# Reciprocal roots of norms computed with tokens in the partitions in a two-block transformer kernel

## What is computed

```python
def rms_norm(x, g):
    return x * lax.rsqrt(jnp.mean(x * x, axis=-1, keepdims=True) + 1e-6) * g

# block 1
mixed = sigmoid(m_gla) * (o_gla @ w_proj_gla) + sigmoid(m_nsa) * (o_nsa @ w_proj_nsa)
x = x + rms_norm(mixed @ w_out, norm_mix_post)            # "second row", norm 2
h = rms_norm(x, norm_ffn_pre)                             # norm 3
x = x + rms_norm((silu(h @ w_gate) * (h @ w_up)) @ w_down, norm_ffn_post)   # norm 4
# block 2
z = rms_norm(x, norm1_g) @ w_in_2                         # norm 5
a, gate, q, k, v = split(z)
y = depthwise_conv31(a * sigmoid(gate)) + bias
y = silu(layer_norm(y, ln_g, ln_b))                       # norm 6, 512 channels
q, k = rms_norm(q per head of 64, q_norm_g), rms_norm(k per head of 64, k_norm_g)
x = x + concat(y, neighbourhood_attention(q, k, v, rpb)) @ w_out_2
x = x + (silu(h2 @ w_gate_2) * (h2 @ w_up_2)) @ w_down_2,  h2 = rms_norm(x, norm2_g)   # norm 7
```

## Time and profile before

| | us |
|---|---|
| three runs | 1563.01, 1563.03, 1564.03 |
| median | 1563.03 |
| profiled execution, whole | 1563.54 |
| its span, first to last instruction | 1561.7 |
| TensorE busy | 1509.5 |
| VectorE busy | 672.1 |
| GpSimd busy | 653.4 |
| ScalarE busy | 588.0 |

### The profile page before, as it was taken

One profiled execution on the slowest core, in us unless ns is written; L12 is line 12 of the kernel. 1 busy time (PEld: TensorE's weight loads), 2 busy tenths in 40 slices (PEclk: granted clock), 3 DMA queues, 4 the chain that ended last, 5 costly groups with the idle time before them and its releaser, 6 DMA issues.

```text
span 1561.7 us, 20183 instructions
## 1 busy us (share of the span) xinstructions
PE 1509.5 (97%) x7270; PEld 1178.8 (75%) x7270; DVE 672.1 (43%) x1095; ACT 588.0 (38%) x906; POOL 653.4 (42%) x302
## 2 busy tenths in 40 slices
PE   7999999999999979999999997999999999999998
PEld 6888788666668847888888885666567888888887
DVE  5212445765553465334331006888736433333001
ACT  4132332744562334223332224566554332222221
POOL 3433312653134424444444552666223444444443
PEclk9999999999999979999999998999999999999999
DMA  5522211111123322333333332322113333333333
GB/s 167 170 82 76 81 46 42 53 41 42 54 56 101 92 63 82 94 96 99 101 94 97 106 108 94 122 68 64 45 41 90 96 97 94 94 94 98 106 106 108
DMA packets 40900, 135.03 MB, mean 86 GB/s; under 512 B 4468, under 2 KB 8824, under 8 KB 40584
## 3 DMA queue, kind: packets, MB, share of 16 engines
q1 hardware_dynamic: 39504, 130.56, 28.1%
q10 hardware_dynamic: 1336, 3.64, 0.8%
HBM read 132.09 MB, written 2.10 MB: 86 GB/s over the span
## 4 chain that ended last, share of the span: by engine, by line
PE 72%; issue 18%; POOL 4%; DVE 3%; ACT 2%; DMA 0%; POOLq 0%; DVEq 0%; SPq 0%; ACTq 0%
PE bank L998 18%; PE bank L1000 18%; PE bank L999 18%; POOL wL L411 3%; PE bank L1027 2%; PE bank L1028 2%; PE bank L1029 2%; PE bank L1259 2%; PE bank L1261 1%; PE bank L1260 1%; DVE bank L1874 1%; PE bank L1152 1%; PE bank L1186 1%; PE bank L1147 1%; PE bank L1254 1%
## 5 line engine op out<-in xcount | busy, mean ns | idle before, releaser
L411 POOL TENSOR_TENSOR wL<-raw,wH 128x1024 fp32r<-128x1024 f32 x235 | 573.3, 2440 | 852.9 <-ACT wH L500 673.9
L500 ACT ACTIVATE wH<-raw 128x1024 fp32r<-128x1024 f32 x209 | 221.4, 1059 | 648.6 <-PE bank L1000 594.1
L998 PE MATMUL bank<-aH,wH 128*128 128x512 f32 x1056 | 420.4, 398 | 25.4 <-DVE aL L1497 18.1
L999 PE MATMUL bank<-aL,wH 128*128 128x512 f32 x1056 | 414.0, 392 | 0.0
L1000 PE MATMUL bank<-aH,wL 128*128 128x512 f32 x1056 | 413.8, 392 | 0.0
L998 PEld LDWEIGHTS bank<-aH,wH 128*128 128x128 f32 x1056 | 199.8, 189 | 81.0 <-issue 27.0
L999 PEld LDWEIGHTS bank<-aL,wH 128*128 128x128 f32 x1056 | 200.0, 189 | 42.4 <-issue 2.0
L1000 PEld LDWEIGHTS bank<-aH,wL 128*128 128x128 f32 x1056 | 200.0, 189 | 42.1
L998 PE MATMUL bank<-fH,wH 128*128 128x512 f32 x352 | 137.3, 390 | 0.0
L999 PE MATMUL bank<-fL,wH 128*128 128x512 f32 x352 | 137.0, 389 | 0.0
L1000 PE MATMUL bank<-fH,wL 128*128 128x512 f32 x352 | 137.0, 389 | 0.0
(11 more groups left out here) (269 smaller groups left out, 1795.1 us busy)
## 6 DMA issues: line engine op xcount, KB each, us to landing
raw<-in_w SPq DMA_DIRECT2D x235, 512.0 KB, 3.5
bmk<-in_bias SPq DMA_DIRECT2D x6, 512.0 KB, 4.8
pj<-in_x SPq DMA_DIRECT2D x4, 512.0 KB, 6.4
out_x<-z2T SPq DMA_DIRECT2D x8, 256.0 KB, 3.6
ct<-in_ct ACTq DMA_DIRECT2D x3, 384.0 KB, 3.2
w1k<-in_w1k ACTq DMA_DIRECT2D x1, 1024.0 KB, 6.4
w1v<-in_w1v ACTq DMA_DIRECT2D x1, 1024.0 KB, 5.1
pv<-in_pv ACTq DMA_DIRECT2D x1, 128.5 KB, 5.6
```

What stands on the lines that cost most here:

```text
L411: pool.tensor_tensor(wL[:, c_slot, :], raw[:, c_slot, :], wH[:, c_slot, :].bitcast(F32), ALU.subtract).then_inc(sem("w_lo"), 1)
L500: act.activation(wH[:, s, :], raw[:, s, :], ACT.Copy).then_inc(sem("w_hi"), 1)
L998: pe.matmul(bank[:], hi, H[:, ka, :], start=(k == 0), stop=False)
L999: pe.matmul(bank[:], hi, L[:, ka, :], start=False, stop=False)
```

## The change

The roots of norms 2, 4 and 6 and the roots of heads are now made with tokens in the partitions. The norms 1, 3, 5 and 7 stay as they are, except that norm 5 is summed in bank 6, since bank 5 is taken.

- `token_sums` makes the squares' tile the weights and one column of ones the moving operand: for each group of 128 tokens one column of 128 sums, 128x4 for all. Ln, Exp and the Newton step (`token_root`) then work on 128x4.
- `spread_root` brings the roots back to the wide form: four transposes of a root column read as 128x128, into a bank that DVE reads in place of nr or lnr.
- The roots of heads are 128x16 (four token groups, q and k, two heads). After DVE's Newton step ACT widens them to hwide, 128x512 for q and for k (`head_roots_wide`), and `head_spread` transposes these. Its first half moves from block 1 to block 2 of its tile. The matrix `spread` and its transfer go.
- Around the LayerNorm, ACT's squares of tiles 2 and 3 stand ahead of a weight split, its root ahead of attention step 10, a weight split behind two of the four Silu; DVE takes a reciprocal between scaling passes and the copy of step 10 behind them.

The diff in its core, in this order: sums and spreads on TensorE; `head_sums`; `head_spread`; the widening and its place in the tiles of in2 on ACT, behind the weight split of the tile; ACT in the LayerNorm; the residual, the narrow root and the LayerNorm on DVE.

```diff
+            def token_sums(out, src, start, stop):
+                for t in range(TT):
+                    mm = pe.matmul(out[:, t:t + 1], src[:, t * P:(t + 1) * P], ones[:, 0:1], start=start and t == 0, stop=stop,
+                                   skip_group_check=True)
+                return mm
             def total_with_last(used, bank):
                 pe.wait_ge(sem("sq_used"), used - 1)
-                pe.matmul(bank[:], ones, ssum[:], start=True, stop=False).then_inc(sem("sq_used"), 1)
+                token_sums(bank, ssum, True, False).then_inc(sem("sq_used"), 1)
                 pe.wait_ge(sem("sq_ready"), used)
-                pe.matmul(bank[:], ones, sq[:, (used - 1) % 2, :], start=False, stop=True).then_inc(sem("sum_ready"), 1)
+                token_sums(bank, sq[:, (used - 1) % 2, :], False, True).then_inc(sem("sum_ready"), 1)
+            def spread_root(n, bank):
+                pe.wait_ge(sem("root_ready"), n)
+                for t in range(TT):
+                    mm = pe.transpose(bank[:, t * P:(t + 1) * P], root[:, t:t + 1].to_broadcast([P, P]), ident)
+                mm.then_inc(sem("root_spread"), 1)
...
             total_with_last(2 * KD, B[4])
+            spread_root(1, B[5])
...
-                pe.matmul(B[6][0:4, :], cst("sel")[:, 0:4], sq[:, 0, :], start=True, stop=False, skip_group_check=True)
-                pe.matmul(B[6][0:4, :], cst("sel")[:, NACH:NACH + 4], sq[:, 1, :], start=False, stop=True,
-                          skip_group_check=True).then_inc(sem("qk_sum"), 1)
+                for of in range(2):
+                    for t in range(TT):
+                        c = 2 * (of * TT + t)
+                        mm = pe.matmul(B[6][:, c:c + 2], sq[:, of, t * P:(t + 1) * P], cst("sel")[:, 0:2], start=True, stop=True,
+                                       skip_group_check=True)
+                mm.then_inc(sem("qk_sum"), 1)
...
                 bank = B[6 if pp < 3 else 4]
+                pe.wait_ge(sem("qk_wide"), 2 * pp + of + 1)
...
-                pe.matmul(bank[:], spread[:, of * P:(of + 1) * P], qkr[:], start=True, stop=True).then_inc(sem("qk_spread"), 1)
+                for t in range(TT):
+                    mm = pe.transpose(bank[:, t * P:(t + 1) * P], hwide[:, of, t, :], ident)
+                mm.then_inc(sem("qk_spread"), 1)
...
+            def head_roots_wide(pp):
+                act.wait_ge(sem("qk_root"), pp + 1)
+                for of in range(2):
+                    act.activation(hwide[:, of].rearrange("p t (h d) -> p t h d", h=2),
+                                   hroot[:, 2 * TT * of:2 * TT * (of + 1)].rearrange("p (t h) -> p t h", h=2).unsqueeze(3)
+                                   .to_broadcast([P, TT, 2, DH]),
+                                   ACT.Copy, scale=(DH ** -0.5, 1.0)[of]).then_inc(sem("qk_wide"), 1)
...
                 if t == 1:
-                    rsqrt(5, B[5], D, (sem("sum_ready"), 5))
+                    rsqrt(5, B[6][:], D, (sem("sum_ready"), 5))
+                if t in SPREAD_AT:
+                    head_roots_wide(SPREAD_AT[t])
...
             act.wait_ge(sem("qk_sum"), 4)
-            for j in range(2):
+            for j in range(4):
                 square(n5 + j, lambda: yT[:, j, :], wait=(sem("ln_cen"), j + 1))
+                if j == 1:
+                    head_roots_wide(3)
             ahead(p, NT2 - 1)
-            for j in range(2, 4):
-                square(n5 + j, lambda: yT[:, j, :], wait=(sem("ln_cen"), j + 1))
             q = PH["out2"]
+            rsqrt(6, narrow(B[7]), S, (sem("sum_ready"), 7), root)
             probabilities(10)
             over_sums(10)
-            rsqrt(6, B[7], S, (sem("sum_ready"), 7), r=lnr)
             probabilities(11)
             act.preload_act_table_set("silu_and_others")
             over_sums(11)
-            ahead(q, 0)
             for j in range(4):
+                if j == 2:
+                    ahead(q, 0)
...
-                    dve.scalar_tensor_tensor(tmp[:, kt % 2, :], src[:, kt, :], vec(gain, kt), nr[:], ALU.mult, ALU.mult)\
+                    dve.scalar_tensor_tensor(tmp[:, kt % 2, :], src[:, kt, :], vec(gain, kt), B[5][:], ALU.mult, ALU.mult)\
...
+            def token_root(n, bank, width):
+                dve.wait_ge(sem("ln_ready"), n)
+                link(dve.tensor_scalar(root_x, narrow(bank), 1.0 / width, EPS, ALU.mult, ALU.add))
+                dve.wait_ge(sem("nr_ready"), n)
+                link(dve.scalar_tensor_tensor(root_t, root, -0.5, root, ALU.mult, ALU.mult))
+                link(dve.tensor_tensor(root_t, root_t, root_x, ALU.mult))
+                dve.scalar_tensor_tensor(root, root_t, 1.5, root, ALU.add, ALU.mult).then_inc(sem("root_ready"), 1)
...
             masked_max(10)
             copied(9)
+            token_root(6, B[7], S)
             over_sums(10)
             normed(3, 0)
-            dve.wait_ge(sem("ln_ready"), 6)
-            link(dve.tensor_scalar(nx[:], B[7][:], 1.0 / S, EPS, ALU.mult, ALU.add))
-            newton(6, r=lnr)
             masked_max(11)
-            copied(10)
+            dve.wait_ge(sem("root_spread"), 3)
             for j in range(4):
                 dve.wait_ge(sem("ln_cen"), 4)
-                dve.tensor_tensor(yT[:, j, :], yT[:, j, :], lnr[:], ALU.mult).then_inc(sem("conv_val"), 1)
-            over_sums(11)
+                dve.tensor_tensor(yT[:, j, :], yT[:, j, :], B[7][:], ALU.mult).then_inc(sem("conv_val"), 1)
+                if j == 1:
+                    over_sums(11)
+            copied(10)
             normed(3, 1)
```

More of the change, by code:

```diff
@@ L307, in two_blocks_kernel, with narrow @@
         B = [ctx.enter_context(nc.psum_tensor(f"bank{i}", [P, S], F32)) for i in range(8)]
+        root, root_x, root_t = (roots[:, i, :] for i in range(3))
+        hroot, hroot_x, hroot_t = (head_roots_[:, i, :] for i in range(3))
+        def narrow(bank):
+            return bank[:, 0:TT]
         def cst(name):
@@ L1249, in _ @@
             total_with_last(4 * KD, B[4])
+            spread_root(2, B[5])
             p = PH["in2"]
```

63 lines of the change are left out of this document (31 added, 32 removed).

## The result

The changed kernel took 1555.56 us in the median of four runs (1554.95 to 1556.39); the kernel before took 1563.53 in the same comparison, a ratio of 0.9946 (0.9929 to 0.9963). The sign and most of the mechanisms were right, the size was not: 8 us instead of 14.2, just outside the range of 1542 to 1555. Later the same kernel had medians of 1553.16, 1555.77 and 1555.18, with single runs between 1551.8 and 1556.4, while the medians of the kernel before stayed between 1563.5 and 1564.3. So the changed kernel also scatters by 4.6 us where the old one had most of its runs within 1.5, and that turned out to be part of the answer.

A forecast was written before the change was run, and what follows sets the result against it. TensorE, busy for 97% of the span, was taken to bound the kernel. Joins 1.6, head sums 0.75, spreads 2.45 and 2.45, LayerNorm 5.65 and clock 1.3 sum to 14.2 us: 1548.8 us forecast, range 1542 to 1555.

The forecast's parts named there:

- two joins: Behind `out1` and `dn1`: narrow sums and root start the first residual step 0.8 us earlier at each, 1.6 us.
- three head sums: Three pairs inside `in2`: sixteen narrow instructions replace two wide products, 0.25 us each, 0.75 us (0.6 to 3.3).
- three first spreads: First spread of each pair in `in2`, moved to block 2: gains 1.55, 0.4 and 0.5, together 2.45 us.
- three second spreads: Second spread of each pair in `in2` (block 5): four transposes replace a wide product, 0.82 us each, 2.45 us.
- LayerNorm with its clock: Convolution's LayerNorm between `in2` and `out2`: 5.65 us from shorter waits plus 1.3 from a higher clock, 6.95.
- The lock: At the joins: a DVE step with two SBUF operands excludes GpSimd's split, so the first narrow step ends near 565.9.
- the wait for ScalarE's widening: First spreads in `in2`: TensorE waits about 0.5 us at block 2 for ACT to widen the 16 roots.
- The rival that it gives most of it back: LayerNorm: waits for step 10's copy and the Silu tiles leave 2.7 instead of 6.95 us; 1553.1 us, chance 0.18.
- the copy of step 10, which was counted: LayerNorm: DVE's copy behind the scaling ends at 1127.1; TensorE in slot 21 waits some 1.6 us for it.
- The clock: TensorE's low clock at and behind the LayerNorm: the second part expected gone, 1.3 us (0 to 2).
- The slower case: Narrow instructions: weight load and product run one behind the other, 0.46 us each; 1573 us, chance 0.04.
- The cheaper case: Narrow steps at the joins slip past the lock and narrow products cost 0.06 us; 1541.8 us, chance 0.08.

The follow-up runs named there:

- joins_wide: Kernel after with both joins as in the kernel before (wide ones products, wide root, no transposes), heads and LayerNorm still narrow: 1555.52 us, ratio 0.9942.
- warm_joins: Kernel after with three extra unused ones products of 512 columns between token sums and root transposes at each join: 1554.26 us, ratio 0.9933.
- f1_copy_first: Kernel after with VectorE's copy of step 11's turned probabilities ahead of the convolution's third and fourth low part: 1552.78 us, ratio 0.9925.
- fill_tile16: Kernel after with two extra unused ones products of 512 columns in the wait ahead of tile 16's head sums: 1553.33 us, ratio 0.9929.

## Where the prediction was right and where it failed

The second execution of the kernel after has no low clock in `in2`; its trace tells the terms of the sum apart. Against the trace of before it gains, in us:

| stretch | forecast | measured |
|---|---|---|
| two joins | 1.6 | 0.44 + 0.43 = 0.9 |
| three head sums | 0.75 | 0.3 |
| three first spreads | 2.45 | 1.55 + 0.28 + 0.41 = 2.2 |
| three second spreads | 2.45 | 2.4 |
| LayerNorm with its clock | 6.95 | 6.8 |
| new wait for the copy of step 11 | none | -1.7 |
| sum (measured: the whole trace) | 14.2 | 10.8 |
| low clock in `in2`, most executions | none | -3.1 |
| scatter ahead of the first join, first trace | none | -0.6 |

The last three lines give the 7.1 us by which the first trace is shorter (1561.7 less 1554.6).

**The joins** failed at the transposes. The lock held as argued: the first step ends with the split. The working then took 0.60 us for four transposes, from a row at full clock, and named the lower clock only as a bound. In the three traces of the kernel before the clock was still full where the transposes would stand (it fell at 567.7 to 568.7), so that the choice had a ground; but all four traces of the kernel after have it at 1.2 GHz there, and `joins_wide`, with the wide sums, too. What the transposes then cost more, 0.45 us at each join, `warm_joins` shows.

**The sums' price** was right, 1.8 us for sixteen, against 2.02 for the two wide ones. Narrow products stand 0.112 us apart in the trace, where the forecast took 0.107. But of the three only the one in tile 11 gained its 0.2; those of tiles 6 and 16 follow a wait of TensorE (0.4 and 1.56 us), and the trace shows no gain there.

**The spreads** came out as worked, the wait for ScalarE's widening too.

**The LayerNorm** gained 6.8 of 6.95 us, over a long chain that was followed step by step. The rival that it gives most of it back came true in one link: not the copy of step 10, which was counted, but the copy of step 11, behind all four low parts. The prediction followed VectorE up to the first low part and stopped there. In the new order ScalarE makes a weight split between the second and the third Silu, so that the third and fourth high part come late, the low parts on VectorE wait for them, and the copy behind these waits too. GpSimd's split, which runs into the third low part, adds some 0.2 us. `f1_copy_first` shows all 1.7 us of it.

**The clock** is the step that failed most. I gave it to the LayerNorm alone, where it did rise as forecast. The sum held nothing for a fall inside `in2`, where the change puts sixteen narrow products behind the waits of tiles 6 and 16. That fall costs 3.1 us in the first trace and none in the second, and the times say that most executions pay it. What decides whether the clock falls there stays open: the experiments move the stretches about, and the nearest to an answer is the one trace of `fill_tile16`, with wide products in the wait and no fall.

The slower case (weight load and product one behind the other) is refuted by the 0.112 us between narrow products. The cheaper case held one true piece: a step past the lock is worth 1.45 us at each join, once its operands allow it.

## What to carry to other kernels

An operation's price isn't only its own duration: products of one or two columns save time on the vector engine, but in most traces TensorE's clock fell at sixteen of them beside a wait, and that cost more in the wide products behind than they saved. It is worth trying to split them up and to keep them away from waits, and their price should be taken at both clocks. When a chain is pulled forward, follow the queue on each engine to its end: the copy that was late stood three operations behind the last one I looked at, behind operands that another engine's new order made late. And profile both kernels several times before stretches of low clock are explained, and compare traces that were alike before the change sets in: one execution showed 7.1 us of gain, the next 10.8.

## What the runs showed of the hardware

- Four fp32 transposes take 0.60 to 0.66 us busy at full clock and 1.12 at 1.2 GHz; narrow fp32 products follow each other every 0.112 us at full clock and every 0.213 at 1.2 GHz. The lower clock doubles them, as it does wide ones (0.23 and 0.43 from start to start).
- TensorE's clock fell 1.6 to 2.1 us behind the last narrow sum of the first join in the four traces of the kernel after, and 4.7 to 5.0 us behind the wide one in the three of the kernel before; but in `joins_wide` it fell 1.9 us behind a wide one (564.09 to 566.0). With three wide products in the gap it fell 5.6 us behind the last of them, with the four transposes between.
- The same kernel has stretches at 1.2 GHz in one execution that it lacks in the next: the kernel after took 1554.6 and 1550.9 us in its first two traces, 3.1 us of it through the stretch behind tile 16.
- A VectorE step on four columns with two SBUF operands took 1.63 us beside GpSimd's split of 2.34; with one operand in PSUM 0.17, beside the same split.
